# Block 1's matrix memory: states ahead of outputs, weighted values from GpSimd, outputs in two buffers

## The reference

```python
def _mlstm_scan(q, k, v, log_i, log_f, state, emit_h):
    def step(carry, inp):
        C, n, m = carry                       # state of the chunk before
        ...
        m_new = jnp.maximum(b_end + m, jnp.max(w_end, axis=1))
        decay = jnp.exp(b_end + m - m_new)
        wk = jnp.exp(w_end - m_new[:, None])
        C_new = decay[..., None, None] * C + jnp.einsum('blh,blhd,blhe->bhde', wk, vf, kf)
        n_new = decay[..., None] * n + jnp.einsum('blh,blhe->bhe', wk, kf)
        if emit_h:
            inter = jnp.exp(a - m_t)
            s = jnp.einsum('bthd,bshd->btsh', qf, kf) * jnp.exp(dmat - m_t[:, :, None])
            num = jnp.einsum('btsh,bshd->bthd', s, vf) + inter[..., None] * jnp.einsum('bhde,bthe->bthd', C, qf)
            den = jnp.sum(s, axis=2) + inter * jnp.einsum('bhe,bthe->bth', n, qf)
            h = num / jnp.maximum(jnp.abs(den), jnp.exp(-m_t))[..., None]
        return (C_new, n_new, m_new), h
    state, hs = lax.scan(step, state, xs)     # forwards over context, then latent; backwards likewise
```

## Time and profile before

| | us |
|---|---|
| three timed runs, median | 1822.85 |
| lowest and highest | 1815.21 and 1823.6 |
| profiled execution, its own time | 1806.77 |
| its span in the trace | 1805.0 |

### The profile page before, as it was taken

The page is one execution under the profiler, slowest core; times in us unless marked ns, Lnnn a source line. Parts: engine busy times, 40 slices in busy tenths (PEclk is TensorE's granted clock), DMA queues, the critical chain, the costliest instruction groups (busy, mean ns, idle before and its releaser), DMA issues.

```text
span 1805.0 us, 19092 instructions
## 1 busy us (share of the span) xinstructions
PE 1574.0 (87%) x7341; PEld 1154.8 (64%) x7341; DVE 1007.2 (56%) x1527; ACT 680.9 (38%) x1081; POOL 296.2 (16%) x278
## 2 busy tenths in 40 slices
PE   5988986779899677799888999888999898989998
PEld 2767762454655434477677777647888676657886
DVE  1318446651457554466465674627777454247776
ACT  2311127211211331456114551124666466335664
POOL 1546620000000000444113441000000042000000
PEclk8899998869899877899688998898999799889999
DMA  8655411200565320666364665307988341039983
GB/s 309 238 160 180 172 47 51 68 1 0 176 238 195 137 94 12 198 211 211 117 168 153 214 215 147 94 0 257 309 297 277 133 157 64 1 118 323 303 289 110
DMA packets 186470, 290.69 MB, mean 161 GB/s; under 512 B 13739, under 2 KB 95115, under 8 KB 186380
## 3 DMA queue, kind: packets, MB, share of 16 engines
q1 hardware_dynamic: 171936, 272.93, 44.7%
q0 software_dynamic: 13200, 13.03, 3.2%
q10 hardware_dynamic: 1244, 3.52, 0.5%
HBM read 287.96 MB, written 1.49 MB: 160 GB/s over the span
## 4 chain that ended last, share of the span: by engine, by line
PE 65%; DVE 21%; ACT 8%; issue 2%; DMA 2%; SPq 1%; POOL 0%; ACTq 0%; DVEq 0%
PE ps L1110 27%; PE ps L2419 13%; DVE P L1791 3%; DVE acc L1833 3%; PE ps L2329 3%; PE ps L1291 2%; ACT ps L1680 2%; DVE PT L1791 2%; PE ps L1272 2%; PE ps L2437 2%; PE ps L2438 1%; PE ps L2439 1%; DVE E L1791 1%; PE ps L1280 1%; DVE small L2025 1%
## 5 line engine op out<-in xcount | busy, mean ns | idle before, releaser
L1110 PE MATMUL ps<-WB,YP 128*128 128x512 f32 x1152 | 279.7, 401 | 19.8 <-DVE WB L1791 19.8
L1110 PEld LDWEIGHTS ps<-WB,YP 128*128 128x128 f32 x1152 | 218.2, 192 | 72.5 <-issue 15.6
L1791 DVE TENSOR_TENSOR WP<-ring,WP 128x2048 fp32r<-128x2048 f32 x96 | 218.8, 2290 | 50.1 <-ACT WP L691 50.0
L1110 PE MATMUL ps<-WP,XP 128*128 128x512 f32 x960 | 233.2, 396 | 8.2 <-DVE WP L1791 8.2
L1110 PEld LDWEIGHTS ps<-WP,XP 128*128 128x128 f32 x960 | 178.8, 189 | 46.0 <-DVE WP L1791 9.3
L691 ACT ACTIVATE WP<-ring 128x2048 fp32r<-128x2048 f32 x96 | 183.3, 1914 | 38.2 <-PE ps L1110 38.2
L2419 PE MATMUL ps<-ring,XT 128*128 128x512 f32 (+3 forms) x448 | 167.3, 530 | 5.5 <-ACT XT L1616 3.3
L562 POOL TENSOR_TENSOR WB<-ring,WB 128x512 fp32r<-128x512 f32 x96 | 133.8, 1396 | 188.9 <-ACT WB L621 188.9
L621 ACT ACTIVATE WB<-ring 128x512 fp32r<-128x512 f32 x192 | 113.9, 628 | 74.9 <-PE ps L1110 72.4
L1833 DVE SCALAR_TENSOR_TENSOR acc<-ring,silu_c,acc 128x512 f32<-128x512 f32 x168 | 138.1, 822 | 5.4
L1791 DVE TENSOR_TENSOR WB<-ring,WB 128x512 fp32r<-128x512 f32 x96 | 85.6, 896 | 97.9 <-ACT WB L621 97.1
(11 more groups left out here) (337 smaller groups left out, 2309.0 us busy)
## 6 DMA issues: line engine op xcount, KB each, us to landing
ring<-in_w_ada SPq DMA_DIRECT2D x72, 1024.0 KB, 7.4
ring<-in_a_w_in SPq DMA_DIRECT2D x36, 1024.0 KB, 5.2
ring<-in_w_gate SPq DMA_DIRECT2D x64, 512.0 KB, 4.5
ring<-in_w_up SPq DMA_DIRECT2D x64, 512.0 KB, 5.6
ring<-in_w_down SPq DMA_DIRECT2D x32, 1024.0 KB, 6.7
ring<-in_w_in SPq DMA_DIRECT2D x24, 1024.0 KB, 7.1
ring<-in_b_w_in SPq DMA_DIRECT2D x12, 1024.0 KB, 5.4
ring<-in_w_out SPq DMA_DIRECT2D x8, 1024.0 KB, 5.1
```

Source lines behind the costliest of these rows:

```text
L1110: ins = mm(dst, x(a), w(b), start=(start and n == 0), stop=(stop_ and n == 2))
L1791: return v.tensor_tensor(out_, a, b, op)
```

## The change

The keys' products of all steps and both directions come first, in one go of 24 matmuls on PE. GpSimd makes the six weighted values of a layer (`VWS`, in VW and in a part of GR that is free then), as soon as the exponentials of the gates are there (`args_exp`). DVE forms the three states one after the other from PSUM, both directions and all heads in one instruction (a copy, then twice a product and a sum), into three tiles, ST and the two halves of VW. Then the outputs: the units (j, d) take turns in two sets of PSUM banks (banks 0 and 1, 4, 6 for even ones, 2 and 3, 5, 7 for odd ones) and of SBUF buffers (halves of PT and E). In round n PE does the scores of unit n, the transposes and the product with the state of unit n - 1, and the numerators of unit n - 2, and DVE the weighting of n, the scaling of n - 1 and the output chain of n - 2. For j = 0 the state is zero, so its product and its scaling are gone. Two of the four squares and sums of heads of layer 1 move from behind the stage into its round 6 (`head_sums`). ACT's copies stay, and with its g_final DMA they no longer wait as before.

```diff
+                pool.wait_ge(S("args_exp"), l + 1)
+                for j in range(3):
+                    for d in range(2):
+                        at = 16 * d + 4 * j
+                        nc.gpsimd.tensor_tensor(VWS[j][:, d], VX[:, tile_of(j, d)], bc(wk[:, at:at + 4], 65), ALU.mult
+                                                ).then_inc(S("vw"), 1)
...
+            def states(l):
+                d5 = decay.rearrange("p (d j a r) -> p r j d a", d=2, j=4, a=2)
+                for r in range(2):
+                    o = slice(64 * r, 64 * r + 64)
+                    link(v.tensor_copy(decay2[o], d5[o, r, 1:3]))
+                dve.wait_ge(S("kv"), l + 1)
+                link(v.tensor_copy(STATES[1], products_of_keys(0)))
+                for j in (1, 2):
+                    link(tt(STATES[j + 1], STATES[j], bc(decay2[:, j - 1], 65), ALU.mult))
+                    ins = tt(STATES[j + 1], STATES[j + 1], products_of_keys(j), ALU.add)
...
+                states(l)
+                for n in range(len(units) + 2):
+                    if n < len(units):
+                        weighted(n)
+                    if 1 <= n <= len(units):
+                        scaled_state(n - 1)
+                    if n >= 2:
+                        normalized(n - 2)
+                    if n == 6 and l == 0:
+                        head_sums(l, (0, 1))
...
+                pe.wait_ge(S("vw"), 6 * l + 6)
+                for j in range(3):
+                    for d in range(2):
+                        for h in range(4):
+                            ins = mm(products_of_keys(j)[head(h % 2), d, h // 2, :],
+                                     P[:, tile_of(j, d), CK + 64 * h:CK + 64 * h + 64], VWS[j][:, d, h, :],
+                                     start=True, stop=True)
+                ins.then_inc(S("kv"), 1)
+                for n in range(len(units) + 2):
+                    if n < len(units):
+                        queries_by_keys(n)
+                    if 1 <= n <= len(units):
+                        transposed(n - 1)
+                    if n >= 2:
+                        numerators(n - 2)
```

More of the change, by code:

```diff
@@ L2222, in block1 @@
                 x3 = P[:, L[0]:L[0] + n, CQ:CK]
[L2223 to L2227, removed]
+                head_sums(l, range(n - 2, n))
                 to("d2a", v.memset(gtmp[:, 0:1], 0.0))
@@ L2246, in block1, with by_half @@
                 c.up("evict", 14)
-            def by_half(d, n):
-                return ps[:, 1024 * d:1024 * d + 1024].rearrange("p (r c) -> p r c", r=2)[:, :, 0:2 * n] \
+            def by_half(n, width):
+                return ps[:, 1024 * (n % 2):1024 * (n % 2) + 1024].rearrange("p (r c) -> p r c", r=2)[:, :, 0:2 * width] \
                     .rearrange("p r (a n) -> p r a n", a=2)
-            def mlstm(l):
[L2254 to L2297, removed]
@@ new lines, in head_sums @@
+            def head_sums(l, tiles):
+                x3 = P[:, 0 if l == 0 else 2:T, CQ:CK]
+                for t in tiles:
+                    e = PTf[:, 520:776].rearrange("p (h d) -> p h d", h=4)
+                    xt = x3[:, t].rearrange("p (h d) -> p h d", h=4)
+                    link(tt(e, xt, xt, ALU.mult))
+                    link(v.reduce_sum(hs[:, 4 * t:4 * t + 4], e, AX.X))
+            def states(l):
[8 more added lines that the diff above has]
+                    ins = tt(STATES[j + 1], STATES[j + 1], products_of_keys(j), ALU.add)
+                    if j == 1:
+                        link(ins)
+                to("states", ins)
@@ L2550, in _, with mlstm, tile_and_rows, queries_by_keys @@
             outp0, gate_sets = [0], [0]
+            def mlstm(l):
+                units, done = mlstm_units(l), 8 * l
+                def tile_and_rows(n):
+                    j, d = units[n]
+                    t = tile_of(j, d)
+                    return slice(128 * t, 128 * t + 128), t, 4 * d + j, d, j
+                def queries_by_keys(n):
+                    cols, _, _, _, _ = tile_and_rows(n)
+                    if n >= 2 and units[n - 2][0] > 0:
+                        pe.wait_ge(S("inter"), from_states(l, n - 2))
+                    for h in range(4):
+                        at = 64 * (h - h % 2)
+                        ins = mm(bank(2 * (n % 2) + h % 2, at, at + 128), MQT[head(h % 2), h // 2, cols],
+                                 MKT[head(h % 2), h // 2, cols], start=True, stop=True)
+                    ins.then_inc(S("qk"), 1)
+                def transposed(n):
+                    cols, _, q, d, j = tile_and_rows(n)
+                    pe.wait_ge(S("z"), done + n + 1)
+                    if n == 0:
+                        pe.wait_ge(S("states"), l + 1)
+                    for h in range(4):
+                        ins = tp(bank(4 + n % 2, 128 * h, 128 * h + 128), ZM[:, q, 128 * h:128 * h + 128])
+                    ins.then_inc(S("z_T"), 1)
+                    if j == 0:
+                        return
+                    for h in range(4):
+                        at = 65 * (h // 2)
+                        ins = mm(bank(2 * (n % 2) + h % 2, at, at + 65), MQT[head(h % 2), h // 2, cols],
+                                 STATES[j][head(h % 2), d, h // 2, :], start=True, stop=True)
+                    ins.then_inc(S("from_state"), 1)
+                def numerators(n):
+                    _, t, _, _, _ = tile_and_rows(n)
+                    pe.wait_ge(S("z_T_sb"), done + n + 1)
+                    if n >= 2:
+                        pe.wait_ge(S("num_used"), done + n - 1)
+                    for h in range(4):
+                        ins = mm(bank(6 + n % 2, 65 * h, 65 * h + 65), E[:, n % 2, 128 * h:128 * h + 128],
+                                 VX[:, t, h, :], start=True, stop=True)
+                    ins.then_inc(S("num"), 1)
+                pe.wait_ge(S("vw"), 6 * l + 6)
+                for j in range(3):
+                    for d in range(2):
+                        for h in range(4):
+                            ins = mm(products_of_keys(j)[head(h % 2), d, h // 2, :],
[7 more added lines that the diff above has]
+                        transposed(n - 1)
+                    if n >= 2:
+                        numerators(n - 2)
```

104 lines of the change are left out of this document (54 added, 50 removed).

## The result

| | before | after |
|---|---|---|
| timed runs, median us | 1819.03 (4 runs) | 1792.55 (4 runs) |
| lowest and highest | 1810.45 and 1823.6 | 1788.63 and 1795.19 |
| ratio, with 95% interval | | 0.9848 (0.9822 to 0.9875) |
| profiled execution, its span | 1805.0 | 1791.0 |
| stage 1: end of the last ada matmul (128 x 1, ahead of the matrix memory on PE) to the memset behind it, us | 54.8 | 44.0 |

By the ratio the change makes the kernel 27.7 us faster (22.7 to 32.4), by the two medians 26.5: the predicted way, and within 3 us of the predicted time of 1790. A second session of six runs gave a median of 1794.22 and a ratio of 0.9826 (0.9799 to 0.9852). The path to the number was in part another one.

What follows compares the result with a forecast made beforehand. PE and DVE taking turns in the two matrix-memory stages was taken as the bound. High-clock savings of 37 us, less 4 for low-clock units, gave 33, so 1822.85 - 33 = 1790 us; range 1777 to 1806 (8 in 10).

Steps and rivals of the forecast that it cites:

- What bounds the kernel: Both matrix-memory stages, 92.0 us together: PE and DVE take turns, PE waiting 17.4 us and DVE 17.6 us.
- DVE's sum and the entry: Layer 1: keys' products to 336.2, states to 338.6, then DVE's rounds of 24.5 us and stalls of 3.3.
- PE's round: PE's work per unit in the matrix-memory stages: 3.2 us at the high clock, 5.0 us at the low.
- Which clock: Matrix-memory stages: two to three units per layer at the low clock, 4 us given back of 37, so 33 us less.
- my own sum for the low clock: Both stages with PE the bound at the low clock, ending at 377.5 and 685.9: 10 + 10 = 20 us less.
- rival 2: Matrix-memory stages: low clock throughout, PE the bound, 20 us less, 1803 us; chance 0.20.
- the forecast's own signs: Matrix-memory stages: 3.1 to 3.5 us between weightings, first near 338.6, memset near 370, second stage 15 us shorter.
- the sum at the high clock: Both stages at 2.4 GHz: layer 1 21 us less, layer 2 16.4 us less, 37 us less together.
- rival 1: Matrix-memory stages: full clock throughout, 37 to 39 us less, 1785 us; chance 0.20.
- the rule that was weighed there: PE in the stages: kept busy without longer gaps, it gets and holds the full clock, giving the whole 37 us.
- Costs of the rest: Outside the stages' sums: GpSimd's products (at worst 8 us), moved head sums, ACT's copies, work behind the stages; taken as nothing.
- The slower rival: Matrix-memory stages: scores only after the previous unit's output chain, 107 against 92 us, 15 us more, 1838; chance 0.03.

Runs made afterwards that it cites:

- values_on_dve: Changed kernel with each layer's six weighted values made by DVE at the start of the stage, not by GpSimd ahead of it; 1788.89 us, ratio 0.9814 to before.
- Filler_4: Changed kernel with four unread dense matmuls added per round, two ahead of the scores and two ahead of the numerators; 1777.64 us, ratio 0.9744 to before.
- filler_start: Changed kernel with unread dense matmuls only ahead of the scores of rounds 0 to 3 and numerators of units 0 and 1; 1777.15 us, ratio 0.9749 to before.
- No_overlap: Changed kernel with units one after the other on PE and DVE, states still first, GpSimd's products kept; 1815.28 us, ratio 0.9952 to before.
- Filler_tail: Changed kernel with four unread matmuls per round, plus 10 behind the last numerators and 14 ahead of the last two transposed tiles; 1777.01 us, ratio 0.9747 to before.

## Why the prediction came out right, step by step

**What bounds the kernel: right.** The turns between PE and DVE were the loss; with them gone the stages lost 23.5 us between the first two traces, and 25.9 between the second ones (94.7 less 68.8).

**DVE's sum and the entry: right.** States done and first weighting at 337.28 with an entry 0.7 us earlier than assumed, against 338.6 foretold (the keys' products took 2.8 and not 3.2). DVE's steps have the durations of before. The head sums are hidden in round 6.

**PE's round: right at each level, save one term.** Foretold 5.0 us low and 3.2 high; measured 5.15 low and, without added work, 2.9 to 3.4 high (values_on_dve). The term that was wrong is the scores: I took 1.04 us at either level, since all four places of layer 1 in the trace showed the same; all four lie where the clock was low. At the high level they take 0.65, and at the low one 1.15 where transposes follow. The keys' products likewise: 24 take 2.8 us low (layer 1 of the changed kernel) and 1.55 high (its layer 2).

**Which clock: wrong.** This is the step that failed. I took two to three units of a layer at the low clock and so gave back 4 us of 37; in the trace all rounds of layer 1 from the third on, and all but the entry of layer 2, are at 0.50. The stages gained 10.8 and 12.7 us where the forecast had 33 in all; my own sum for the low clock was 10 and 10. Layer 2 is better than that mostly by its entry, whose keys' products and first scores ran at 2.4 GHz. So the mechanism was rival 2's, PE-bound at the low clock, and not the forecast's. The signs written down beforehand say the same: rounds of 5 us at 0.50 were rival 2's sign, and of the forecast's own signs the 3.1 to 3.5 us between weightings, the memset near 370 (it came at 376.0) and the second stage 15 us shorter all failed. Filler_4 shows that the sum at the high clock was sound: 39.2 us against 37, rival 1 says 37 to 39. What I had in hand was the row of 365 to 370, a PE busy throughout at 0.50; I read it as an exception, and without added work it was what nine of ten stages of the new order did. The trace after disagrees with the rule that was weighed there (the Trainium skill, "TensorE: Matmul & The Clock Gate", "Why this matters for your kernels") as to getting the full clock by being busy: PE was busy for 32.2 us at 0.50 in the changed kernel. It agrees as to keeping it: once there the full clock held for 14.4 us of dense rounds in filler_start and for 20 us in values_on_dve.

**Why the time was right nevertheless.** The stages give 23.5 to 26 us, the timed runs 27.7 (22.7 to 32.4) and, in the second session, 31.7 (27.0 to 36.6) by the ratio and 28.7 by the medians. The end stretch varies by 12 us from trace to trace with either order, and the start of the first stage by 7 (329.9 to 336.8), and a mix of short and long executions moves a median of a few runs by several us. Whether that is the whole of the 2 to 6 us between is not settled. The closeness to 1790 is luck. Of the 33 us foretold the stages gave 23.5, and the 27.7 of the timed runs lies just under the forecast's own 28 to 36; some 4 us came from time that no stage shows, and the median of before, from which the 33 were taken off, came out at 1819.03 and not at 1822.85.

**Costs of the rest: right.** GpSimd held nobody (maxima 10.05 us), hardly anything was given back behind the stages (from layer 1's first output matmul to the second stage 256.2 us against 255.4), and the gate transposes, late next at the low clock, left the stretch from the memset to the first output matmul as it was (15.4 against 15.2 in layer 1, 9.0 against 8.6 in layer 2).

**The slower rival** needed scores behind the output chain. No_overlap is nearly that and costs 90.3 us for both stages, 7.5 a unit with the entries, under the 107 foretold, because PE still runs one unit's scores beside DVE's chain.

## What to carry to other kernels

Before pricing small matmuls, look up the granted clock at each place where their duration was read: equal durations at several places may only mean that all of them were at one level. Removing a wait does not bring the high clock by itself; a stage of small matmuls can stay at 1.2 GHz while PE is never idle, and twelve dense matmuls at the entry of each stage, into columns nobody reads, made the two stages 16 us shorter here on top of the change's 24, in the one trace taken; its timed runs agree (ratio 0.9749). To tell an order's worth from the clock's, compare units that ran at the same level. Two traces of the same kernel should be compared stretch by stretch before a difference between two kernels is explained.

## What the runs showed of the hardware

- The granted clock had two lasting levels in the same rounds: 0.50 for 32.2 us of a PE that was never idle (after), 1.00 for 20 us (values_on_dve) and for 14.4 us (filler_start) without added work. Filler_tail shows the low one even with added work (layer 2, 0.53).
- The same code behind the stages took 1099.2 to 1111.6 us over fourteen traces, and the longer it took, the longer its clock had stood at 1.2 GHz (163 to 187 us).
- From one start to the next, four scores (float32, 64 rows by 128 columns) took 1.15 us at 1.2 GHz and 0.65 at 2.4 ahead of transposes; four numerators (128 rows, 65 columns) 1.9 and 1.04 to 1.09.
- GpSimd's product of 128 x 260 took 0.6 us, and VectorE's maxima from PSUM beside it were not slowed.
